# The first ada pieces as TensorE products in four strips, the first value projection in half-megabyte pieces

## What is computed

```python
c_act = silu(c)
mod = c_act @ ada_w[0] + ada_b[0]              # 1024 -> 6 * 1024
sh_m, sc_m, g_m, sh_f, sc_f, g_f = split(mod, 6)
h = rms_norm(x, pre_mix_g[0]) * (1 + sc_m) + sh_m
z = gelu(h @ a_w_in + a_b_in)                  # 1024 -> 4096
u, v = split(z, 2)
v = layer_norm(v)                              # over all 2048 values
v = tril(w_s) @ v + b_s                        # per group and chunk of 128 tokens
y = (u * v) @ a_w_out
...
```

## Time and profile before

| | |
|---|---|
| three executions | 1787.51, 1792.65 and 1787.19 us, median 1787.51 |
| profiled execution, span from first to last instruction | 1791.7 us (the profile gives no other time of it) |
| TensorE busy | 1722.3 us, 96% of the span |
| VectorE busy | 1159.6 us, 65% |
| ScalarE busy | 894.2 us, 50% |
| mean granted TensorE clock | 0.986 of full speed |
| bytes moved | 363.43 MB, mean 203 GB/s |

### The profile page before, as it was taken

One profiled execution on the slowest core, in us unless ns is written; L12 is line 12 of the kernel. 1 busy time (PEld: TensorE's weight loads), 2 busy tenths in 40 slices (PEclk: granted clock), 3 DMA queues, 4 the chain that ended last, 5 costly groups with the idle time before them and its releaser, 6 DMA issues.

```text
span 1791.7 us, 22029 instructions
## 1 busy us (share of the span) xinstructions
PE 1722.3 (96%) x8926; PEld 1437.3 (80%) x8926; DVE 1159.6 (65%) x1611; ACT 894.2 (50%) x1268; POOL 7.4 (0%) x20
## 2 busy tenths in 40 slices
PE   5899999999989999999999979999999999999998
PEld 4798788878867888888888857888888889778887
DVE  7779878779766754565546976554665556675553
ACT  3555644465566444454445566444554445574442
POOL 0000000000000000000000000000000000000000
PEclk8999999999989999999999999999999999999999
DMA  8966777766624665555455324555554556345451
GB/s 342 394 242 260 268 298 291 295 250 253 252 78 146 254 223 176 209 194 186 175 188 200 118 71 153 188 176 181 196 210 177 176 203 232 118 140 184 173 197 47
DMA packets 54117, 363.43 MB, mean 203 GB/s; under 512 B 5744, under 2 KB 8944, under 8 KB 13056
## 3 DMA queue, kind: packets, MB, share of 16 engines
q1 hardware_dynamic: 52256, 351.47, 53.8%
q0 software_dynamic: 1760, 10.56, 1.4%
HBM read 360.95 MB, written 1.05 MB: 202 GB/s over the span
## 4 chain that ended last, share of the span: by engine, by line
PE 83%; DVE 10%; ACT 3%; DMA 3%; issue 1%; POOL 0%; SPq 0%; DVEq 0%; ACTq 0%
PE pp L603 80%; DVE low L1772 3%; DVE raw L1785 2%; PE pp L853 2%; DMA raw<-in_w 2%; DMA cst<-in_csts 1%; PE pp L785 1%; ACT wh L1267 1%; DVE hf L1916 1%; PE pp L930 1%; DVE tb L1772 1%; DVE x L1775 0%; DVE hl L1772 0%; ACT Pb L1505 0%; DVE tb L1775 0%
## 5 line engine op out<-in xcount | busy, mean ns | idle before, releaser
L1772 DVE TENSOR_TENSOR low<-raw,wh 128x2048 fp32r<-128x2048 f32 (+3 forms) x340 | 637.9, 1891 | 361.4 <-ACT wh L1267 360.9
L1267 ACT ACTIVATE wh<-raw 128x2048 fp32r<-128x2048 f32 (+3 forms) x346 | 536.0, 1568 | 440.3 <-PE pp L603 292.2
L603 PE MATMUL pp<-wh,hh 128*128 128x512 f32 x1312 | 523.9, 399 | 12.7 <-ACT hh L1297 7.6
L603 PE MATMUL pp<-low,hh 128*128 128x512 f32 x1312 | 515.8, 393 | 7.4 <-DVE low L1772 7.3
L603 PE MATMUL pp<-wh,hl 128*128 128x512 f32 x1312 | 509.3, 393 | 4.3 <-DVE hl L1772 4.3
L603 PEld LDWEIGHTS pp<-wh,hh 128*128 128x128 f32 x1312 | 248.9, 190 | 69.9 <-issue 13.8
L603 PEld LDWEIGHTS pp<-low,hh 128*128 128x128 f32 x1312 | 249.1, 190 | 59.1 <-DVE low L1772 9.7
L603 PEld LDWEIGHTS pp<-wh,hl 128*128 128x128 f32 x1312 | 248.6, 190 | 59.0 <-DVE hl L1772 6.0
L603 PE MATMUL pp<-wh,hidh 128*128 128x512 f32 x592 | 232.0, 392 | 0.0
L603 PE MATMUL pp<-low,hidh 128*128 128x512 f32 x592 | 230.6, 389 | 1.0 <-DVE low L1772 1.0
L603 PE MATMUL pp<-wh,hidl 128*128 128x512 f32 x592 | 230.6, 389 | 0.0
(11 more groups left out here) (205 smaller groups left out, 1162.3 us busy)
## 6 DMA issues: line engine op xcount, KB each, us to landing
raw<-in_w SPq DMA_DIRECT2D x314, 1024.0 KB, 4.8
raw<-in_w SPq DMA_DIRECT2D x24, 768.0 KB, 4.4
gain<-in_w POOLq DMA_DIRECT2D x6, 512.0 KB, 4.8
bT<-in_rel POOLq DMA_DIRECT2D x1, 2048.0 KB, 11.6
cst<-in_csts POOLq DMA_DIRECT2D x1, 1029.0 KB, 19.6
xT<-in_xT SPq DMA_DIRECT2D x1, 1024.0 KB, 7.2
binr<-in_bin POOLq DMA_DIRECT2D x1, 1024.0 KB, 10.7
wsT<-in_ws POOLq DMA_DIRECT2D x1, 1024.0 KB, 15.0
```

What stands on the lines that cost most here:

```text
L603: return e.matmul(out, lhsT, rhs, start=start, stop=stop, skip_group_check=True)
L1267: q.then_inc(e.activation(wh[j % NW][:, c], raw[i % NRAW][:, c], ACT.Copy), s_wh, (j, part))
L1772: return e.tensor_tensor(out, a, b, op)
```

## The change

**The first eight ada pieces** leave the ring. They load into buffers of their own (`first_w`: five in the area of the later hidden values, one beside xT, one in the place of x and one in the place of cst) with the rows of ada_w on the partitions. c comes as one row, eight tiny products turn it into columns, and `c_cols` holds each column of silu(c) beside 31 columns of zeros. For each piece `ada_partial` multiplies eight k tiles in plain float32, 128 x 32 stationary by 128 x 256 moving, into four strips of 32 PSUM partitions, two k tiles per strip. ScalarE copies the [128, 256] result to SBUF (`partial_copy`), two products against a column of ones sum the strips (`ada_sum`), and VectorE adds the bias (`mod_of`).

**The first three value groups** come in pieces of two k tiles, [128, 1024], in four rounds j of three groups. Round j needs h tiles 2j and 2j + 1. In rounds 0 to 2 the strips and sums of the next two ada pieces stand between the products.

**The norm** takes half of its squares on VectorE and becomes exp(-0.5 ln(...)) on ScalarE. **GpSimd** issues `binr`, `wsT`, `tri` and `bsb` only after the last strips and the last piece of group 2, masks `wsT` itself, and loads `cst` and `x` when the first piece of the second u group has come. The broadcast of c to `cact` comes after the twelfth piece, and its silu after round 3. The later ada pieces start two matrix pieces later in the stream.

The diff, cut to its core:

```diff
@@ stream
+            thin = name == "a_v" and gi < 3
+            for k0, k in [(2 * j, 2) for j in range(4)] if thin else k_pieces(kt) if width(parts) > 128 else [(0, kt)]:
...
-    early, late = main[0:6:2], main[1:6:2]
-    items = [ada[4], ada[0], early[0], ada[5], ada[1], early[1], ada[6], ada[2], early[2], ada[7], ada[3], *late]
-    ada, main = ada[8:], main[6:]
-    marks = [(0, 0), (6, 4), (18, 12), ...
+    items = [main[4 * g + j] for j in range(4) for g in range(3)]
+    first, ada, main = ada[:8], ada[8:], main[12:]
+    marks = [(0, 0), (2, 0), (8, 4), (18, 12), ...
@@ tensor_program
+            def ada_partial(c):
+                b, before = firstp.begin(("first", c), (s_mod, ("mod", c)))
+                if before:
+                    q.wait_ge(*before)
+                q.wait_ge(s_first[c], 0)
+                for half in range(2):
+                    for j in range(4):
+                        k = 2 * j + half
+                        ins = mm(b[32 * j:32 * j + 32, 0:T], c_cols[:, k, :], first_w[c][:, k, :], half == 0, half == 1)
+                q.then_inc(ins, s_part, c)
+            def ada_sum(c):
+                b = firstp.of(("first", c))
+                q.wait_ge(s_copied, c)
+                for i in range(2):
+                    ins = mm(b[:, T + i:T + i + 1], first_sum[c // 4][:, 128 * i:128 * i + 128], ones[:, 0:1], i == 0, True)
+                q.then_inc(ins, s_sum, c)
...
+            ada_partial(4)
+            first_squares()
+            ada_partial(0)
+            ada_sum(4)
+            ada_sum(0)
...
+            for j in range(3):
+                for g in range(3):
+                    for k in range(2):
+                        for m in range(2):
+                            first_products(j, g, k, m)
+                        if (g, k) == (0, 1):
+                            ada_partial(5 + j)
+                        if (g, k) == (1, 1):
+                            ada_partial(1 + j)
+                            ada_sum(5 + j)
+                        if (g, k) == (2, 0):
+                            ada_sum(1 + j)
@@ scalar_program
+            for j in range(1, 4):
+                partial_copy(4 + j)
+                ahead.upto(3 * j)
+                partial_copy(j)
+                ahead.upto(3 * j + 1)
+                first_h((2 * j, 2 * j + 1))
+                ahead.upto(3 * j + 2)
@@ vector_program
+            first_h(0, lambda: None)
+            ahead.upto(2)
+            for j in range(1, 4):
+                ahead.upto(3 * j + 1)
+                first_h(j, lambda: ahead.upto(3 * j + 2))
...
-            q.then_inc(tt(wsT[:, :, :], wsT[:, :, :], bc4(tri[:, :], 16), ALU.mult), s_side, "tri")
@@ sync_program
+                if i in (0, 3, 6, 9):
+                    for c in (4 + i // 3, i // 3):
+                        o = first_off[c]
+                        e.dma_start(first_w[c][:, :, :], ...).then_inc(s_first[c].sem, 16)
@@ pool_program
-            first = pieces[of_group[("a_v", 0)][1]]
-            q.wait_ge(s_raw[first % NRAW], first // NRAW)
+            last = pieces[of_group[("a_v", 2)][-1]]
+            q.wait_ge(s_part, 3)
+            q.wait_ge(s_raw[last % NRAW], last // NRAW)
...
+            q.then_inc(e.tensor_tensor(wsT[:, :, :], wsT[:, :, :], bc4(tri[:, :], 16), ALU.mult), s_tri, 0)
```

More of the change, by code:

```diff
@@ L322, in build @@
         small = sb("small", [128, 64])
+        first_w = [place(f"firstw{i}", [128, 8, T], F32, big + 8192 * i) for i in range(5)]
+        first_w.append(place("firstw5", [128, 8, T], F32, side + 8192))
+        first_w += [x[:, :, :].rearrange("p a (k t) -> p (a k) t", t=T), cst[:, 0:2048].rearrange("p (k t) -> p k t", t=T)]
+        first_sum = [gain[:, 256 * i:256 * i + 256] for i in range(2)]
+        c_cols = gain[:, 512:768].rearrange("p (k m) -> p k m", k=8)
         v = place("v", [128, 2, 2048], F32, big)
@@ L438, in build @@
         misc = Ring([bank[6], bank[7]])
+        firstp = Ring([bank[7], bank[6]])
         s_r, t_r, o_r = Ring([bank[2], bank[3]]), Ring([bank[4], bank[5]]), Ring([bank[6], bank[7]])
-        rings = [ta, tb, Sb, Pb, PT, rl, pairs, fillp, ixp, misc, s_r, t_r, o_r]
+        rings = [ta, tb, Sb, Pb, PT, rl, pairs, fillp, ixp, misc, firstp, s_r, t_r, o_r]
         every, _ = stream()
-        items = [it for it in every if it[0] != "rows"]
+        items = [it for it in every if it[0] not in ("rows", "first")]
+        first_off = {it[6]: it[1] for it in every if it[0] == "first"}
         row_off = {it[6]: it[1] for it in every if it[0] == "rows"}
@@ L452, in build @@
         s_raw = [signal(f"raw{i}_landed") for i in range(NRAW)]
[L453 removed]
+        s_ld = {n: signal(n + "_landed") for n in ("c", "col", "xT", "x", "cst", "tri", "c_row", "ws", "bin", "bs", "rel")}
+        s_first = {c: signal(f"first{c}_landed") for c in range(8)}
+        s_part, s_copied, s_sum = signal("ada_partial"), signal("partial_copied"), signal("ada_sum")
+        s_vsq, s_tri = signal("squares_dve"), signal("tri_taken")
         s_gain = signal("gain_landed")
@@ L1607, in odd_fill @@
                 yield from out_steps("odd_out")
+            q.wait_ge(s_part, "c")
+            q.wait_ge(s_set, "c_cols")
+            q.then_inc(e.activation(c_cols[:, :, 0:1], bank[5][:, 0:8].unsqueeze(2), ACT.Silu), s_cact, "columns")
+            log_tables()
+            for i in range(2):
+                first_squares(i)
+            partial_copy(4)
+            first_root()
+            partial_copy(0)
+            ahead.upto(0)
+            first_h((0, 1))
+            ahead.upto(2)
[6 more added lines that the diff above has]
+                ahead.upto(3 * j + 2)
             q.wait_ge(s_ld["c"], 0)
             q.then_inc(e.activation(cact[:, :], cact[:, :], ACT.Silu), s_cact, "cact")
[L1612 to L1622, removed]
             def gelu_v(g):
@@ L2237, in odd_fill, with mod_of, first_h @@
                 yield from out_steps("odd_out")
-            def first_h(j):
+            def mod_of(c):
+                q.wait_ge(s_sum, c)
+                q.wait_ge(s_ld["col"], 0)
+                o = COL["ada_b"] + 2 * c
+                q.then_inc(tt(mod[:, 2 * c:2 * c + 2], firstp.of(("first", c))[:, T:T + 2], col[:, o:o + 2], ALU.add), s_mod, ("mod", c))
+                s_mod.at["sec", c // 4] = s_mod.n
+            def first_h(j, between):
                 c = slice(2 * j, 2 * j + 2)
-                q.wait_ge(s_mod, ("mod", 4 + j))
+                mod_of(4 + j)
+                mod_of(j)
                 q.wait_ge(s_mod, ("mod", j))
                 q.then_inc(stt(der[:, 0, c], modcols(1)[:, c], 1.0, pcols("pre_mix_g", 0)[:, c], ALU.add, ALU.mult), s_side, ("der0", j))
[L2245 to L2260, removed]
+                first_h_of(j, der[:, 0, :], (s_side, ("der0", j)), between)
+            q.wait_ge(s_ld["xT"], 0)
+            for i in range(2, 4):
+                t = slice(2 * i, 2 * i + 2)
+                q.then_inc(tt(ta.bufs[1][:, 2 * i - 4:2 * i - 2, :], xT[:, t, :], xT[:, t, :], ALU.mult), s_vsq, ("x0", i))
+            first_h(0, lambda: None)
+            ahead.upto(2)
+            for j in range(1, 4):
+                ahead.upto(3 * j + 1)
+                first_h(j, lambda: ahead.upto(3 * j + 2))
             def spatial_bias(g):
@@ L2533, in build @@
             s.at = {0: 16}
-        s_ld["cst"].at = {0: 32}
+        for s in s_first.values():
+            s.at = {0: 16}
         s_out.at = {"all": 64}
```

96 lines of the change are left out of this document (57 added, 39 removed).

## The result

The changed kernel takes 1802.54 us (median of 5 executions, 1799.39 to 1806.22) against 1787.51 (5 executions, 1785.48 to 1794.36). The ratio is 1.0072, 95% interval 1.0054 to 1.0090: slower by 12.9 us on 1787.5, between 9.7 and 16.1. The forecast was 1798.5 in a range of 1786 to 1812.

A forecast was written before the change was run, and what follows sets the result against it. TensorE, busy 96% of the span, was taken as the bound. Terms 0.25 + 7.8 + 5.1 + 2.0 - 4.1 + 0 = 11.05; 11.0 put on the median 1787.5 gave 1798.5 us, range 1786 to 1812.

The forecast's parts named there:

- The likeliest case: The forecast itself, chance 0.50: ada pieces leave VectorE but another engine still paces h; 11.0 us slower, 1798.5 us.
- The start: Up to the second value product: it can start at 22.7 us against 22.45, so +0.25 us.
- The strips: Strips of six ada pieces in TensorE's stream behind 22.7 us, hidden by nothing: +7.8 us.
- P: TensorE's time for the strips of one ada piece: 1.3 us, with 0.95 to 2.4 as its ends.
- 3.8 in the rival: Strips on TensorE gain nothing: 3.8 us per ada piece, +20 us on top, 1818 us; chance 0.10.
- The case of 4.3 us more: Every change of shape drains TensorE: 16 changes at 0.27 us each, 4.3 us more, 1803 us; chance 0.10.
- The crossing: From round to round: TensorE waits 3.7 us at each of three, 11.1 us in place of 6.0, +5.1 us.
- The clock: Slow clock behind the waits between rounds: 1.6 to 1.7 us each, 5.1 in place of 3.1, +2.0 us.
- the rival of the half hidden crossing: Between rounds, waits shorter or clock holding: 3 x 1.4 to 3 x 3 us, total 1787 to 1793; chance 0.20.
- The saving: At the fourth value group, the 2.5 us wait and its 1.6 us of slow clock go: -4.1 us.
- Later ada pieces: Two matrix pieces later in the stream, waits may go or come: between -1.9 and +4.9 us, taken as 0.
- The hidden crossing: Between rounds, hl is there when TensorE comes and the clock stays up: -7.4 us, 1780; chance 0.10.

The follow-up runs named there:

- e5: The changed kernel with all eight k tiles of an ada piece in one strip of 32 PSUM partitions instead of four; ratio to the kernel before 1.0168.
- e1: The changed kernel with VectorE making both hl of a round ahead of splitting the third half piece; ratio to the kernel before 1.0002.
- e2: The changed kernel with ScalarE rounding one half piece more before each copy of strips and before hh; ratio to the kernel before 1.0017.
- e6: The kernel before with the mask waiting for tri and wsT alone, and cst and x loaded late; ratio to the kernel before 0.9973.
- e3: The changed kernel with both order edits, VectorE's hl ahead of the third split and ScalarE's earlier roundings; ratio to the kernel before 1.0000.
- e9: The changed kernel with hl ahead of the third split and the mask product back on VectorE behind the first bias; ratio to the kernel before 1.0039.

## Why the prediction was right

**Side and size.** Slower by 11.0 was forecast; 12.9 (9.7 to 16.1) was measured, and 11.4 by the start of the transposes. The likeliest case came about in its mechanism: the chain over ScalarE and VectorE, the waits for `hl` at the third product of rounds 1 to 3, and no wait at the fourth group. That the total came so close is in part luck, since its terms were off in both directions. At the transposes it was too low by 5.1 us in the start, the slow stretch of round 0, the crossings and the later ada pieces, and too high by 4.7 us in the clock, the strips and the saving. The three value groups ended at 79.6 and not at about 82.

- **The start (+0.25 forecast).** The second product started at 23.63 against 22.45: +1.2. The squares took 5.56 us in place of 4.5, and the strips ahead of them 1.86 in place of 1.3. The slow spacing lasted through the whole first group of round 0, eleven products and not eight. The term was too small by 0.9 us, and the slow stretch by 0.6. The steps as written down end at 22.25 and not at 22.7 (17.8, then 1.8 to the first `hh`, then 2.65), so the sum itself had put in 0.45 too much, and the steps were short by 1.4.
- **The strips (+7.8).** 1.0 us from first start to next start at 43.44, and about 0.2 more where products give way to strips and come back (43.12 to 43.44 and 44.44 to 44.78, against 0.23): six at 1.2 are 7.2. P (1.3) was close, and the price of a row without overlap, 3.8 in the rival, measured 3.6 in e5. The case of 4.3 us more, 0.27 at each change of shape, did not come about: these rows leave some 0.1 us for each. TensorEngine Tiling (Array Packing) of the Trainium skill, Key Properties, has a drain at each change of mode; the trace allows one, but no longer than this.
- **The crossing (+5.1).** From the end of the strips to the first `hl` product 7.18 us stood against 7.4 to 7.5, the chain of steps as written down. The waits are 2.5 us (0.31 and 2.21) and not 3.7: the chain is 0.3 shorter, the sums take 0.84 us of TensorE's time per crossing and not 0.6 (33.77 to 34.24 and 35.71 to 36.08), and the rest is products that start late behind a sum or a wait. The term has a slip: the sums were taken off the wait and then called covered, though TensorE still spends them. What a crossing costs is its whole length less its fourteen products of 0.2275, which is 4.3 by the forecast's own steps, so three less the 6.0 of before are +6.9 and not +5.1. Measured it is 4.0 each, so +6.0. e1 and e2 show the place: about 9 and 6.9 us back.
- **The clock (+2.0).** One of three waits was followed by the slow spacing, not three: about 1.5 us in place of 5.1, so this term was -1.6 instead of +2.0. This was the largest error in the opening, and on the other side of the start's and the crossing's. Here the trace has what the rival of the half hidden crossing named, a clock that holds: waits and slow clock together are 3.0 us per crossing, the upper end of that rival. The time did not go to its 1793, since the sums, the start and the later ada pieces came on top. Executions of the changed kernel have mean clocks of 0.985 to 0.992 and times of 1806.2 to 1799.4 in the same order, which fits a number of slow stretches that differs from one execution to the next; only one of them has a trace.
- **The saving (-4.1).** e6 measured it by itself: -4.6 at the ones product, -4.8 by time (interval 3.0 to 6.6).
- **Later ada pieces (0, between -1.9 and +4.9).** From the products by v to the transposes: 80.6 us before, 83.3 changed. +2.7, within the ends; the 0 was too low. The wait that I had thought might go went, and one of 2.08 came a piece later. The waits of the whole stretch are 1.1 us longer, and the rest fits the slow clock behind the 2.08 (0.57). The clock is not the cause, though: e1 has clock 1.00 there, two waits of 0.98 and 1.36 at the places 149.25 and 161.80, and the same 83.3.
- **GpSimd's mask (0).** It started at 76.47 and took 5.3 us; nothing waited for it, since TensorE reached the ones product at 85.09.

**The rivals.** The hidden crossing is what e1 and e3 are: all three waits gone, and yet the time is only level with before, not 7.4 us below it. Its sum left out the later 2.7 and 0.6 of the start (23.29 in e1), kept the clock up in round 0 as well, took 0.95 for strips that cost 1.2 and 1.8 for sums that cost 2.5, and had no wait of 0.31 for `hh`. So even in the best of the orders tried this change gives back on TensorE what it takes from VectorE. That the ada pieces leave VectorE and something else paces h was the forecast's core, and the trace shows it: VectorE is busy for 1.45, 5.5, 5.6 and 5.6 us in the windows 0 to 20, 20 to 30, 30 to 45 and 45 to 60, where it had 8.2, 9.6, 14.5 and 10.9.

## What to carry over

Moving work from an engine that is busy to the one that sets the time pays only if the waits on the first engine were longer than the work; count the moved work on the receiver at its own price before anything else. Where three engines hand a value around once per round, write down each engine's list between two hand-overs and put nothing in it that waits for something queued behind the hand-over elsewhere: one line of order was worth about 9 us here. And look for the part of a change that needs none of the rest: a mask that waits only for what it reads, with the late-needed loads issued later, was the only gain, and it could be had alone. Before a load is moved, look at which of the loads its reader waits for.

## What was not expected of the hardware

GpSimd's mask product and VectorE's split of a [128, 2048] piece ran at the same time, and both became slow. GpSimd's timeline in the changed kernel:

```profile
76.47 5.33 POOL L2590 TENSOR_TENSOR wsT<-wsT,tri 128x2048 f32<-128x2048 f32 x1 [9.21 <-DMA tri<-in_csts]
```

and VectorE's:

```profile
75.01 2.28 DVE L1840 TENSOR_TENSOR low<-raw,wh 128x2048 fp32r<-128x2048 f32 x1
...
78.73 5.21 DVE L1840 TENSOR_TENSOR low<-raw,wh 128x2048 fp32r<-128x2048 f32 x1 [0.24 <-ACT wh L1323]
```

The split takes 5.21 us beside it and 2.28 otherwise; in e1 it is 4.75. GPSIMD Engine Reference of the Trainium skill, Key points, states contention with VectorE instructions that have two SBUF inputs; the trace agrees. Its section 3.1 gives 4497 ns on GpSimd for an add of two tensors of 2048 float32 columns; the mask product of that size took 5.33 us here and 4.64 in e1, each time with a split of VectorE beside it for part of it. In e9, with the mask on VectorE, the next split is back at 2.28. The wait for `hl` of 2.21 us came three times, to the hundredth, and the clock fell behind one of them only. Behind the later wait for `low` it is the same: 2.08 us in the changed kernel was followed by clock 0.57, and 2.09 us in e1 by 1.00. Why the one and not the other, these runs do not show. An order with strips for only some of the pieces, so that neither TensorE nor VectorE is the bound of the opening, was not tried, and neither was the kernel before with a semaphore of its own for `tri` and nothing else.
